# RWKV chunk matrices of a hybrid mixer: pairs of 32-token chunks as 64 by 64 blocks in 64-row array tiles

## What is computed

```python
def step(state, inp):
    r_t, w_t, k_t, v_t, kk_t, a_t = inp
    sa = jnp.einsum('bhvk,bhk->bhv', state, -kk_t)
    state = (state * w_t[:, :, None, :] + sa[..., None] * (kk_t * a_t)[:, :, None, :]
             + v_t[..., None] * k_t[:, :, None, :])
    return state, jnp.einsum('bhvk,bhk->bhv', state, r_t)
```

## Time and profile before

| | |
|---|---|
| median of 3 timed runs | 2121.88 us (2121.46 to 2122.12) |
| profiled execution | 2135.11 us |
| its span, first to last instruction | 2133.8 us |
| mean granted TensorE clock | 0.940 |
| busy in the span | PE 89%, DVE 39%, ACT 30%, POOL 2% |
| slowest core | the only one |

### The profile page before, as it was taken

How to read it: one execution, slowest core, us unless ns; L and a number is a source line. 1 busy time by engine, 2 the same in 40 slices (tenths; PEclk the granted TensorE clock), 3 DMA queues, 4 the chain that set the end, 5 groups by cost and what they waited for, 6 DMA issues and landing times. The chain is left out here.

```text
span 2133.8 us, 41370 instructions
## 1 busy us (share of the span) xinstructions
PE 1892.1 (89%) x17744; PEld 1332.8 (62%) x17744; DVE 830.4 (39%) x1665; ACT 635.1 (30%) x1197; POOL 52.1 (2%) x58
## 2 busy tenths in 40 slices
PE   7999998999987886789999999588866999999995
PEld 6889998889986784644444444267855444444432
DVE  5766666666654375521111111233745111111112
ACT  4554445554433232311111111132423111111112
POOL 0400000400000000000000000000000000000000
PEclk9999999999998997799999999888977999999998
DMA  6235553345513312699999999422117999999992
GB/s 262 100 139 184 192 181 132 110 149 193 182 60 103 101 42 79 260 383 426 429 428 428 428 428 428 190 80 92 31 80 308 384 427 428 428 428 428 430 426 115
DMA packets 52332, 540.00 MB, mean 253 GB/s; under 512 B 6576, under 2 KB 7760, under 8 KB 14672
## 3 DMA queue, kind: packets, MB, share of 16 engines
q1 hardware_dynamic: 52176, 537.80, 63.0%
HBM read 536.73 MB, written 1.05 MB: 252 GB/s over the span
## 5 line engine op out<-in xcount | busy, mean ns | idle before, releaser
L2668 PE MATMUL experts_psG<-weights_gu,experts_xc 128*64 128x512 f32 x2048 | 454.5, 593 | 19.5 <-DMA weights_gu<-in_moe_up 19.5
L2668 PEld LDWEIGHTS experts_psG<-weights_gu,experts_xc 128*64 128x64 f32 x2048 | 146.9, 137 | 315.6 <-issue 277.2
L422 DVE TENSOR_TENSOR ring_low<-ring_raw,ring_high 128x1024 fp32r<-128x1024 f32 x180 | 224.3, 1248 | 158.3 <-ACT ring_high L416 158.2
L2693 PE MATMUL experts_psD<-weights_d,experts_hT 128*64 128x512 f32 x1024 | 233.9, 598 | 1.6 <-ACT experts_hT L2629 1.6
L416 ACT ACTIVATE ring_high<-ring_raw 128x1024 fp32r<-128x1024 f32 x180 | 189.1, 1054 | 155.0 <-PE ffn_ps L539 91.3
L537 PE MATMUL ffn_ps<-first_x_high,ring_high 128*128 128x256 f32 x704 | 199.0, 283 | 0.1
L2599 DVE SCALAR_TENSOR_TENSOR experts_yc_low<-experts_psD,experts_slot_gate,experts_yc_high 128x512 fp32r<-128x512 f32 x64 | 48.0, 751 | 387.7 <-ACT experts_yc_high L2632 387.7
L539 PE MATMUL ffn_ps<-first_x_high,ring_low 128*128 128x256 f32 x704 | 198.6, 282 | 0.0
L538 PE MATMUL ffn_ps<-first_x_low,ring_high 128*128 128x256 f32 x704 | 198.0, 281 | 0.0
L2589 DVE TENSOR_TENSOR experts_sig<-experts_sig,experts_psG 128x256 f32<-128x256 f32 x64 | 27.0, 421 | 370.0 <-ACT experts_sig L2620 370.0
L2620 ACT ACTIVATE experts_sig<-experts_psG 128x256 f32<-128x256 f32 x64 | 24.6, 384 | 420.1 <-PE experts_psG L2668 420.1
(11 more groups left out here) (487 smaller groups left out, 3234.0 us busy)
## 6 DMA issues: line engine op xcount, KB each, us to landing
weights_gu<-in_moe_gate SPq DMA_DIRECT2D x64, 2048.0 KB, 25.1
weights_gu<-in_moe_up SPq DMA_DIRECT2D x64, 2048.0 KB, 29.5
weights_d<-in_moe_down SPq DMA_DIRECT2D x64, 2048.0 KB, 28.4
ring_raw<-in_w SPq DMA_DIRECT2D x90, 1024.0 KB, 4.9
mix_w_raw<-in_w_in SPq DMA_DIRECT2D x44, 512.0 KB, 3.7
output_w_raw<-in_w_out SPq DMA_DIRECT2D x8, 1024.0 KB, 8.1
mix_w_raw<-in_w_in SPq DMA_DIRECT2D x4, 528.0 KB, 5.4
const<-in_const SPq DMA_DIRECT2D x1, 1344.0 KB, 17.7
```

The lines of the kernel that those rows point to most:

```text
L422: dve.tensor_tensor(self.low[:, n % AHEAD], self.raw_half(n), self.high[:, n % AHEAD], ALU.subtract)\
L2668: ins = pe.matmul(out, xc[:, kk], wgu[:, place, kk, :, j * S:(j + 1) * S], start=kk == 0, stop=kk == DT - 1)
L2693: ins = pe.matmul(psD[rows, :], hT[:, c, j * SLOTS:(j + 1) * SLOTS], wd[:, place, 2 * j + c, i * 512:(i + 1) * 512], start=j == 0 and c == ...
```

## The change

Two neighbouring chunks are held as one 64 by 64 matrix. The masks are built over 64 by 64 and are zero outside the two diagonal 32 by 32 blocks, so that products of such matrices keep the chunks apart; the values are the same as before. Every matmul of products, squares, inverse, through and read_out now takes a pair: half as many, each with 64 columns, on array positions (64q, 64q), or (64g, 64q) and (64q, 64g). The arrays mN, mX, mM double. PSUM is laid out anew: the squares use banks 0 and 1 (one before), the inverse bank 5 (1 before), all four token transposes share bank 4 (4 and 5 before), and are issued one to a unit: (0) after products(2), (1), (2) and (3) in GA, GQ and GK. Masks and the copies of squares take twice the columns. states_and_ends and the state chain keep their 32-row tiles. The constant c_ident goes; three mask constants grow from 32 to 64 columns.

```diff
-    within, local = np.arange(P)[:, None] % C, np.arange(C)[None, :]
+    within, local = np.arange(P)[:, None] % 64, np.arange(64)[None, :]
+    chunk = within // C == local // C
...
-             ("c_below", within > local), ("c_above", within < local), ("c_upto", within <= local),
+             ("c_below", chunk & (within > local)), ("c_above", chunk & (within < local)), ("c_upto", chunk & (within <= local)),
...
-        mN = st.sb("mN", [P, 2, 2, U, C])
-        mX = st.sb("mX", [P, U, C])
-        mM = st.sb("mM", [P, 3, U, C])
+        C2, HPB = 2 * C, CPB // 2
+        mN = st.sb("mN", [P, 2, 2, U, C2])
+        mX = st.sb("mX", [P, U, C2])
+        mM = st.sb("mM", [P, 3, U, C2])
...
-        pair_of = lambda i: (0, i * P) if i < 2 else (2, (i - 2) * P)
+        by_half = lambda a: a.rearrange("p a (b q c) -> p q (a b) c", b=SB, q=HPB)
+        pair_of = lambda i: (0, i * NP * C2) if i < 2 else (2, (i % 2) * NP * C2)
...
-                    dve.tensor_tensor(flat(mX[:]), flat(mX[:]), ps[:, 1, 0:U * C], ALU.add).then_inc(inv_updated, 1)
+                    dve.tensor_tensor(flat(mX[:]), flat(mX[:]), ps[:, 5, 0:U * C2], ALU.add).then_inc(inv_updated, 1)
...
-                    act.activation(mN[:, (j + 1) % 2, 0:n].rearrange("p i u c -> p (i u c)"), ps[:, 0, 0:n * U * C], ACT.Copy)\
+                    act.activation(mN[:, (j + 1) % 2, 0:n].rearrange("p i u c -> p i (u c)"), ps[:, 0:n, 0:U * C2], ACT.Copy)\
...
-                        for j in range(CPB):
-                            cols = slice(blk * P + C * j, blk * P + C * (j + 1))
+                        for q in range(HPB):
+                            cols = slice(blk * P + C2 * q, blk * P + C2 * (q + 1))
...
-                                                tile_position=(64 * g, C * j))
+                                                tile_position=(64 * g, C2 * q))
...
                 def transposes(i, src):
-                    if i >= 2:
-                        pe.wait_ge(tok_copied, i - 1)
+                    if i >= 1:
+                        pe.wait_ge(tok_copied, i)
...
                     for u in range(U):
-                        for j in range(CPB):
-                            ins = body(u, slice(C * j, C * (j + 1)), (C * j, C * j))
+                        for q in range(HPB):
+                            ins = body(u, slice(C2 * q, C2 * (q + 1)), (C2 * q, C2 * q))
...
-                        for j in range(CPB):
-                            r, at = slice(C * j, C * (j + 1)), (blk * HEADS + h) * 64
+                        for q in range(HPB):
+                            r, at = slice(C2 * q, C2 * (q + 1)), (blk * HEADS + h) * 64
...
-                                    u, at = of_head(h, blk), (C * j, 64 * g)
+                                    u, at = of_head(h, blk), (C2 * q, 64 * g)
```

More of the change, by code:

```diff
@@ L1737, in inverse @@
                         pe.wait_ge(inv_updated, j)
-                    chunks(lambda u, r, at: pe.matmul(ps[r, 1, u * C:(u + 1) * C], mN[r, (j + 1) % 2, 0, u], mX[r, u],
+                    chunks(lambda u, r, at: pe.matmul(ps[r, 5, u * C2:(u + 1) * C2], mN[r, (j + 1) % 2, 0, u], mX[r, u],
                                                       start=True, stop=True, tile_position=at)).then_inc(inv_done, 1)
@@ L1743, in through @@
                     for h, blk in heads_blocks:
[L1744 to L1745 removed]
+                        for q in range(HPB):
+                            r, at = slice(C2 * q, C2 * (q + 1)), (blk * HEADS + h) * 64
                             ins = pe.matmul(ps[r, dst, at:at + 64], m[r, of_head(h, blk)], src[r, blk, h],
[L1747 removed]
+                                            start=True, stop=True, tile_position=(C2 * q, C2 * q))
                     return ins
@@ L1781, in read_out @@
                             pr, blk = n // SB, n % SB
[L1782 to L1783 removed]
+                            for q in range(HPB):
+                                r = slice(C2 * q, C2 * (q + 1))
                                 for g in range(2):
                                     h, out = 2 * pr + g, slice(64 * g, 64 * g + 64)
[L1786 removed]
+                                    u, at = of_head(h, blk), (C2 * q, 64 * g)
+                                    to = ps[out, 2 + q, (what * NP + n) * C2:(what * NP + n + 1) * C2]
                                     if what == 0:
[L1788 to L1789 removed]
+                                        ins = pe.matmul(to, W[2][r, blk, h], mM[r, 1, u], start=True, stop=True, tile_position=at)
                                     elif what == 1:
[L1791 to L1794 removed]
+                                        pe.matmul(to, W[1][r, blk, h], mM[r, 1, u], start=True, stop=False, tile_position=at)
+                                        ins = pe.matmul(to, tok[r, 3, blk, 64 * h:64 * h + 64], mM[r, 2, u],
+                                                        start=False, stop=True, tile_position=at)
                         ins.then_inc(rp_done, 1)
@@ L1841, in after @@
                         products(2, K_, A_)
+                        transposes(0, F[:, A_])
                     elif u == GA:
@@ L1844, in after @@
                         inverse(0)
-                        transposes(0, F[:, A_])
                         transposes(1, F[:, B_])
@@ L1849, in after @@
                         inverse(1)
+                        transposes(2, F[:, K_])
                         pe.wait_ge(wa_loaded, 16)
@@ L1859, in after @@
                         products(4, K_, R_)
-                        transposes(2, F[:, K_])
                         transposes(3, v_)
```

30 lines of the change are left out of this document (14 added, 16 removed).

## The result

| | before | after |
|---|---|---|
| median of 4 timed runs each, same chip | 2121.67 us (2118.86 to 2122.12) | 2093.36 us (2091.37 to 2099.09) |
| profiled execution | 2135.11 us | 2095.04 us |
| its span | 2133.8 us | 2093.7 us |
| mean granted TensorE clock | 0.940 | 0.951 |

The direction was right, the size too small.

What follows compares the result with a forecast made beforehand. TensorE bounds the kernel, losing time to stops for instruction blocks and a lowered clock. Stops -17.2, clock -6 and rows +6.2 sum to -17.0 us, taken off the 2121.9 median: 2105 us, range 2096 to 2118.

Steps and rivals of the forecast that it cites:

- The count of instructions: In stage_mix2: PE stops waiting for its next block of 256 instructions; 1408 fewer per pass end such stops.
- The six stops whose end was forecast: Three stops per pass, in the inverse and products(3) and (4), go: 7.2 + 10.0 = 17.2 us given back.
- The cost of the rows: Fewer but dearer 64x64 matmul rows in products, squares, inverse, through, read_out: +3.1 us per pass, +6.2 for both.
- I leave its cost and its slow clock as they are: The stop after products(1), 2.64 and 2.57 us, moves 128 instructions on into squares(0), its cost kept.
- one of two kinds that stay: Stops expected to remain: the one after products(1), and the one in states_and_ends (2.15 us).
- The clock: Projection units after the stops run 6.9 us over; 6 us of that was expected back.
- within what was allowed: The states_and_ends stop stays; new block boundaries there can cost or save about 2.5 us per pass, put into the range.
- -17.0: Forecast change of the whole time in us: -17.2 for stops, -6 for the clock, +6.2 for rows.
- The rivals: Four alternatives: low clock, stops tied to their places (2128 us, chance 0.08), no tile overlap, bad block boundaries.
- The clock did not stay low: Rival: longer tile work between units keeps the clock low, losing the 6 us or more: 2111 to 2118, chance 0.20.
- The diagonal tiles overlap: Rival denied this: rows in the touched stretch at 60 ns instead of 30, 2132 us, slower; chance 0.03.
- The boundaries fell badly: Rival: two new stops of 2.5 us per pass, a slow unit behind each: about 2121, no change; chance 0.05.

Runs made afterwards that it cites:

- e1: Kernel before with 32 tiny matmuls (128 instructions) added per pass ahead of the touched part: 2123.43 us against 2117.61, ratio 1.0030.
- e8: Kernel after with 16 small 32x32 matmuls ahead of each of 19 batches, 1216 instructions more per pass: 2120.31 us, 1.0002 against the kernel before.
- e9: Half of the change: squares, inverse and N in 64-row tiles, masked products, through(3) and read_out as before: 2113.98 us against 2118.08 for the kernel before, 0.9985.
- e5: Kernel after, unchanged, run again on another chip: 2096.68 us, 0.9884 against the kernel before.
- e2: Kernel after with the weight loads of units 16 and 17 asked for earlier: 2088.99 us, 0.9849 against the kernel before.
- e7: Kernel before with the weight loads of units 16 and 17 asked for earlier: 2119.50 us, 0.9996 against the kernel before.
- e4: Kernel after with six more 0.5 MB weight loads, two asked for at once, the others as earlier ones landed: 2101.13 us, one run.
- e10: Kernel after with three more 0.5 MB weight loads, all asked for at once behind that of a projection unit: 2096.32 us, one run.
- e3: Kernel after with each pair matmul of products, squares, inverse and through preceded by a 4-column one of the same operands: 2128.96 us, 1.0051 against the kernel before.

## Why the prediction was off

**The count of instructions: right.** The six stops whose end was forecast are gone, x1359 is x750, and e1, e8 and e9 put stops where the count says. The Trainium skill ("Runtime: NRT & Kernel Launch", section Instruction fetch mechanics), which calls the crossing into a new block mostly hidden, does not hold here: in the kernel before PE waited 1.9 to 4.2 us at such a crossing wherever the block before it was done in less than 3 us. It does hold there for blocks of 3.7 us and more, among them all that contain most of a projection unit: 0.5 us at most.

**The cost of the rows: right.** Forecast +3.1 us per pass. Measured: squares and inverse 11 batches x 0.34 = +3.8 (0.96 against 0.62 us from start to start, the mean of ten batches of before at the full clock), products 160 x 14.5 ns = 2.3 against 2.8, so -0.5, through +0.1 and read_out 1.70 against 2.44 us, so -0.7: +2.7. DVE's masks took 0.69 us and ACT's copies of 128x1024 1.02; nothing waited for them. One sum of the forecast does not come out: with its own lower rows (27 and 9 ns) the low end for both passes is +1, not +3; nothing hangs on it.

**"I leave its cost and its slow clock as they are", of the stop after products(1): this step failed.** I had read the stop after products(1) as one of two kinds that stay, and moved it into squares(0). It was of the same kind as the other three. products(0) and (1) of before are 128 rows, with their weight loads 256 instructions, and the block was entered with their first, at 685.04 us: it held these 1.3 us of work and nothing else; its packet moved at 686.53 and PE went on at 688.98. I did the sum of instructions for the later units and not for this one. After, the two products are 128 instructions, every block there holds most of a projection unit, and the stop went in both passes: 2.64 + 2.57 = 5.2 us. The clock had stood at its lower level for 3.41 us behind each (690.06 to 693.47 and 1423.92 to 1427.34), which is another 3.4 us for both; the unit's 5.30 us are 3.72 now.

**The clock: right in kind, sized too small.** I counted the excess of five projection units, 6.9 us, and took 6. The granted clock of before stood at 1.2 GHz for 10.2 us of the first stretch and 20.5 of the second, in seven places. Two of them and the sum of all seven:

```profile
703.71:707.12 3.41, 3.41 (x44) 3.17 (x45) 1.30 (x3) 1.20 (x2) 0.00 (x0) 0.50 0.03 7
1437.58:1444.40 6.82, 4.93 (x47) 4.34 (x48) 1.30 (x3) 1.20 (x2) 0.00 (x0) 0.50 0.01 2
...
sum 30.73, PE 27.26 PEld 22.95 DVE 7.60 ACT 7.52 POOL 0.00; mean PE 3.89 PEld 3.28 DVE 1.09 ACT 1.07 POOL 0.00
```

PE worked for 27.3 of these 30.7 us, at half speed, so 13.6 us were lost, and after the change no part of the stretches is at the lower level. 3.4 of the 13.6 lie behind the first stops just named; of the other 10.2 I had taken 6. What I had left out of the excess is work between the units, such as the second half of an inverse and the transposes behind it in the first row, that ran at half the clock as well. The windows agree: the two stretches lost 118.8 - 89.3 = 29.5 us, of which 22.4 were idle and 13.6 clock; that leaves 6.5 us of work gained in both passes without read_out, 3.2 each, where the rows above say 3.4.

**states_and_ends: within what was allowed.** The stop stays, 2.80 and 2.61 us. In the first pass it was 2.15, with one of 0.48 ahead of it at 742.54, and in the second 1.89:

```profile
1485.63 0.37 PE L1768 MATMUL mix_ps<-mix_W,mix_tok 32*64 32x64 f32 x3 [1.89 <-issue]
```

The packet now falls into the queued loads, and the clock now falls behind the stop in the first pass too. From the first row of states_and_ends to that of read_out it was 8.4 and 9.0 us and is 9.7 and 9.6: +2.0 for both passes.

**Together:** -17.0, less 5.2 for the first stops, 7.6 for the clock (13.6 in place of 6) and 1.7 for the work (6.5 in place of 8.2 without read_out), plus 2.0 for states_and_ends and 0.5 for what follows it (-1.5 in place of -2.0) is -29.0. From the first projection unit to the last row of stage_mix2 the two traces show 131.3 us down to 120.2 and 138.1 down to 120.1, which is -29.0. The rest of the 40 us between the two profiled executions lies in code that is the same in both, 5.4 of it ahead of the mixer. The medians differ by 28 and by 23, since the profiled execution of before was 13 us over its median. Such stops vary with what the weight loads do at the time: 2.30 and 4.18 us at one instruction in the two passes of before, 2.61 us in after and 3.72 in e5 at one instruction of one kernel. I took the full stops of one slow execution off a median, which was probably too much by a few us, and left out 13 that this execution had (5.2 and 7.6); what is seen in the medians is the sum of both errors. How much the stops cost in an execution of median length no profile here shows.

**The rivals.** None came true. The clock did not stay low: up to 4.1 us of tile work and transposes between two units (697.9 to 702.05 us) went by at 1.00. The diagonal tiles overlap, 28.5 to 30 ns a row. The boundaries fell badly only in e9.

## What to carry to other kernels

Idle TensorE with "issue" as its releaser, inside a batch of small matmuls, is worth a count: if the stops lie whole multiples of 256 instructions apart, weight loads and semaphore waits counted, fewer and larger instructions pay more than the row costs say. The stops cost more than their own time: here 22.4 us of them brought 13.6 us of slow clock. Count through the whole stage, the first block too, and look at each block's own duration: in the kernel before those done in under 3 us stopped PE by 1.9 us or more, those of 3.7 us and more by 0.5 at most (1.2 in e1, in a block of 4.0 us beside queued loads). When the last such stops remain behind queued DMA loads, asking for some loads earlier can remove them, as in e2, where the block ahead took 10.1 us; in e7, where it took 4.5, it did not.

## What the runs showed of the hardware that was not expected

- A fetch of instructions is put off by queued loads: the packet moved 1.3 to 1.9 us later with three or four loads of 0.5 MB asked for and not yet landed (e4, e10). One load of 0.5 MB was enough where it got ahead of the fetch: 3.3 us from entry to packet in place of 0.9, and a stop of 4.18 us in place of 2.30 (before, second and first pass).
- After a packet had moved, PE went on 2.2 to 2.7 us later (726.66 to 728.84, 700.93 to 703.64 in before), so where a block holds only small matmuls the next one is there 3.6 to 4.5 us after the entry into it, and up to 5.5 us when a load comes in between (1433.97 to 1439.47).
- A stop of 2 to 4 us can lower the clock for what follows: 0.53 in the 3.6 us behind that of states_and_ends, after 45 us at 1.00. Without the stop (e2) the same work ran at 1.00. Not every stop does: behind those of 1.89 us (715.34) and 2.15 us (746.27) in the first pass of before it stayed at 1.00.
- A change of the tile size costs about 0.1 us on PE (e8), and two matmuls on the same place with different columns follow each other instead of overlapping (e3: four and four rows in 0.23 us, where four of 64 columns alone take 0.12).
